# The first loads and transposes of a two-layer decoder step, put in another order on three queues

## What is computed

```python
q, k, v, z, xbc, dt = jnp.split(x @ w_in, IN_SPLITS, axis=-1)
dt = jax.nn.softplus(dt + dt_bias)
lam = jnp.exp(jnp.dot(lp[0], lp[1])) - jnp.exp(jnp.dot(lp[2], lp[3])) + lam_init
...
mk, mv = jnp.split(mem_prompt @ w_ckv[l], 2, axis=-1)
hp = _layer_norm(DEEPNORM_ALPHA * hp + _cross_attn(hp, mk, mv, w_cq[l], w_co[l]), ln_g[l, 1], ln_b[l, 1])
```

## Time and profile before

| | |
|---|---|
| median of 3 runs | 1859.1 us (1857.46 to 1862.97) |
| the profiled execution: its own time | 1857.33 us |
| its span, first to last instruction | 1855.5 us |
| mean granted TensorE clock | 0.969 |
| busy in the span: PE, DVE, ACT, POOL | 94%, 66%, 46%, 5% |
| DMA | 454 MB, mean 245 GB/s |

### The profile page before, as it was taken

One profiled execution on the slowest core, in us unless ns is written; L12 is line 12 of the kernel. 1 busy time (PEld: TensorE's weight loads), 2 busy tenths in 40 slices (PEclk: granted clock), 3 DMA queues, 4 the chain that ended last, 5 costly groups with the idle time before them and its releaser, 6 DMA issues.

```text
span 1855.5 us, 23939 instructions
## 1 busy us (share of the span) xinstructions
PE 1736.1 (94%) x8736; PEld 1355.2 (73%) x8736; DVE 1225.2 (66%) x1708; ACT 854.7 (46%) x978; POOL 100.1 (5%) x114
## 2 busy tenths in 40 slices
PE   7999997989998999998788999999999999999994
PEld 4646575689997555476477888888888888888883
DVE  2685627155543287534527979798988989797982
ACT  1122221054432131202115777676777777676762
POOL 0620000000000431000000000000000000000000
PEclk9999998999998999999898999999999999999996
DMA  9567536745535264553683989899999999998950
GB/s 323 169 213 237 220 123 242 254 137 182 171 117 194 91 217 148 214 200 115 241 255 125 351 263 368 307 356 335 332 359 316 362 313 380 296 367 308 354 208 26
DMA packets 298980, 454.07 MB, mean 245 GB/s; under 512 B 10710, under 2 KB 213648, under 8 KB 298886
## 3 DMA queue, kind: packets, MB, share of 16 engines
q1 hardware_dynamic: 294022, 440.47, 69.3%
q0 software_dynamic: 2576, 8.38, 1.5%
q10 hardware_dynamic: 2304, 4.20, 0.6%
HBM read 440.77 MB, written 12.38 MB: 244 GB/s over the span
## 4 chain that ended last, share of the span: by engine, by line
PE 86%; DVE 7%; ACT 3%; issue 1%; DMA 1%; SPq 1%; ACTq 0%; POOL 0%; DVEq 0%
PE bank L1142 83%; PE bank L1146 3%; DVE arena L2558 1%; DVE ring_low L2041 1%; ACT high L1669 1%; DMA out<-mem_rows 1%; ACT L1669 0%; ACT arena L1732 0%; ACT ye_high L1705 0%; DVE st L2530 0%; DVE st L2451 0%; DVE R L2172 0%; ACT xT L1768 0%; SPq L717 0%; DVE pair_in L2191 0%
## 5 line engine op out<-in xcount | busy, mean ns | idle before, releaser
L2041 DVE TENSOR_TENSOR ring_low<-ring,high 128x2048 fp32r<-128x2048 f32 x264 | 602.8, 2291 | 93.8 <-ACT high L1669 85.9
L1669 ACT ACTIVATE high<-ring 128x2048 fp32r<-128x2048 f32 x264 | 505.6, 1918 | 107.2 <-PE bank L1142 106.2
L1142 PE MATMUL bank<-high,xg_high 128*128 128x512 f32 x704 | 281.9, 400 | 8.7 <-DVE ring_low L2041 7.0
L1142 PE MATMUL bank<-ring_low,xg_high 128*128 128x512 f32 x704 | 275.1, 391 | 0.0
L1142 PE MATMUL bank<-high,xg_low 128*128 128x512 f32 x704 | 274.3, 390 | 0.0
L1142 PEld LDWEIGHTS bank<-high,xg_high 128*128 128x128 f32 x704 | 132.2, 188 | 35.1 <-DVE ring_low L2041 8.4
L1142 PEld LDWEIGHTS bank<-ring_low,xg_high 128*128 128x128 f32 x704 | 132.1, 188 | 28.6
L1142 PEld LDWEIGHTS bank<-high,xg_low 128*128 128x128 f32 x704 | 132.5, 188 | 25.3
L1732 ACT ACTIVATE arena<-bank 128x512 f32<-128x512 f32 (+3 forms) x95 | 47.4, 526 | 220.2 <-PE bank L1142 146.8
L1142 PE MATMUL bank<-high,he_high 128*128 128x512 f32 x352 | 139.7, 397 | 0.0
L1142 PE MATMUL bank<-ring_low,he_high 128*128 128x512 f32 x352 | 137.4, 390 | 0.0
(11 more groups left out here) (318 smaller groups left out, 2472.1 us busy)
## 6 DMA issues: line engine op xcount, KB each, us to landing
ring<-in_w_exp_gu SPq DMA_DIRECT2D x176, 1024.0 KB, 11.4
ring<-in_w_exp_down SPq DMA_DIRECT2D x40, 2048.0 KB, 14.0
ring<-in_w_in SPq DMA_DIRECT2D x12, 2048.0 KB, 11.8
ring<-in_w_ffn_gu SPq DMA_DIRECT2D x22, 1024.0 KB, 8.0
ring<-in_w_ckv SPq DMA_DIRECT2D x8, 2048.0 KB, 8.2
ring<-in_cache_mem_k SPq DMA_DIRECT2D x16, 1024.0 KB, 8.1
ring<-in_cache_mem_v SPq DMA_DIRECT2D x16, 1024.0 KB, 6.4
ring<-in_cache_attn_k SPq DMA_DIRECT2D x32, 256.0 KB, 4.2
```

Of the source, the lines that this page charges most:

```text
L1142: return M.matmul(out, lhsT, rhs, start=start, stop=stop)
L1669: S.activation(high_bufs[h % HIGH_BUFS][:], ring[:, s, j * HALF:(j + 1) * HALF], ACT.Copy).then_inc(split_high, 1)
L2041: V.tensor_tensor(ring_low[:, s, part], ring[:, s, part], high_bufs[h % HIGH_BUFS][:], ALU.subtract).then_inc(split_low, 1)
```

## The change

SP now loads the identity alone first (semaphore `ident_landed`), then x, then the q columns; the rest of the constants, the six vector DMAs, the memory rows and the page table follow behind q. The nine DMAs of `small_landed` are issued by POOL, the dt columns first, in front of its wait for `const_landed`. PE transposes x first, then `vraw`; the memory rows are transposed behind the two q tiles. The entries of `xin` are emptied by DVE (0, 2, 4) and ACT (1, 3). The memory rows' ring slot stands behind q's.

```diff
@@ psum_groups
-    g = [(("vec",), "V")]
-    g += [(("xin", n), "V") for n in range(5)] + [(("mem", n), "A") for n in range(4)]
+    g = [(("xin", n), "A" if n in (1, 3) else "V") for n in range(5)] + [(("vec",), "V")]
...
+                if l == 0 and c == "q" and t == DECODE_FIRST[-1]:
+                    g += [(("mem", n), "A") for n in range(4)]
@@ sync
-            sp.dma_start(const[:], a["consts"]).then_inc(const_landed, 16)
+            sp.dma_start(const[:, C_ID:C_ID + P], a["consts"][:, C_ID:C_ID + P]).then_inc(ident_landed, 16)
             s = rg.claim(sp, ("x",))
...
                 columns((l, "q"), w_in, 0)
                 if l == 0:
-                    for i, n in enumerate(("dt_bias", "a_log", "d_skip")):
-                        sp.dma_start(raw8[:, i], a[n].partition_broadcast(P)).then_inc(small_landed, 16)
...
+                    first_vectors()
+                    memory_rows()
@@ gpsimd
             G.memset(xpad[:, :, 0:3], 0.0).then_inc(buffers_set, 1)
+            for n in range(L):
+                pool.dma_start(wdt[:, n], a["w_in"][n, :, 3072:3080].rearrange("(k p) n -> p k n", p=P)
+                               ).then_inc(small_landed, 16)
+            for i, n in enumerate(("dt_bias", "a_log", "d_skip")):
+                pool.dma_start(raw8[:, i], a[n].partition_broadcast(P)).then_inc(small_landed, 16)
+            with nc.allow_non_contiguous_dma(reason="sixteen words"):
+                for i, n in enumerate(("dt_bias", "a_log")):
+                    pool.dma_start(col8[:, i, :], a[n].rearrange("l h -> h l")).then_inc(small_landed, 16)
+            pool.dma_start(lraw, a["lambda_params"].partition_broadcast(P)).then_inc(small_landed, 16)
+            pool.dma_start(wr[:], a["w_router"][0].rearrange("(k p) n -> p k n", p=P)).then_inc(small_landed, 16)
             pool.wait_ge(const_landed, 16)
@@ tensor
-            pe.wait_ge(const_landed, 16)
+            pe.wait_ge(ident_landed, 16)
+            blocks8(("xin",), slot(("x",))[:, 0:3072].rearrange("p (t n) -> p t n", t=3))
             pe.wait_ge(vecs_landed, 16 * 6)
             bk = turns.open(pe, ("vec",))
...
+            pe.wait_ge(const_landed, 16)
+            copied(pe, ("xin", 3))
             pe.wait_ge(buffers_set, 6)
...
+                    if l == 0 and c == "q":
+                        memory_columns()
```

More of the change, by code:

```diff
@@ L690, in _, with first_vectors, memory_rows @@
                          ).then_inc(landed[s], 16)
[L691 to L694, removed]
+            def first_vectors():
+                sp.dma_start(const[:, C_ID + P:NCONST], a["consts"][:, C_ID + P:NCONST]).then_inc(const_landed, 16)
+                for j, (src, r0) in enumerate((
+                        (a["ln_g"].rearrange("l i (k n) -> (l i k) n", n=P), 0),
+                        (a["ln_b"].rearrange("l i (k n) -> (l i k) n", n=P), 48),
+                        (a["ssm_norm_w"].rearrange("l (k n) -> (l k) n", n=P), 96),
+                        (a["attn_norm_w"], 104),
+                        (a["conv_b"].rearrange("l (k n) -> (l k) n", n=P), 106))):
+                    sp.dma_start(vraw[r0:r0 + src.shape[0], 0, :], src).then_inc(vecs_landed, 16)
+                sp.dma_start(vraw[0:64, 1, :], a["conv_w"].rearrange("l i (k n) -> (l i k) n", n=P)
+                             ).then_inc(vecs_landed, 16)
+            def memory_rows():
+                s = rg.claim(sp, ("mem",))
+                sp.dma_start(ring[:, s, 0:2048].rearrange("p (t n) -> p t n", t=2),
+                             a["mem_prompt"].rearrange("o (t p) n -> p (o t) n", p=P)).then_inc(landed[s], 16)
+                sp.dma_start(ptab[:], a["page_table"].rearrange("b g -> (b g)").unsqueeze(0)).then_inc(ptab_landed, 16)
             def columns(key, w, c0):
@@ L1235, in _, with memory_columns @@
             full(tr(bk[:, 128:192], vraw[0:64, 1, :], 64))
[L1236 to L1243, removed]
+            def memory_columns():
+                mem_in = slot(("mem",))[:, 0:2048].rearrange("p (t n) -> p t n", t=2)
+                for n in range(4):
+                    bk = turns.open(pe, ("mem", n))
+                    for j in range(4):
+                        k = 4 * (n % 2) + j
+                        last = tr(bk[:, j * P:(j + 1) * P], mem_in[:, n // 2, k * P:(k + 1) * P], P)
+                    full(last)
+            pe.wait_ge(const_landed, 16)
+            copied(pe, ("xin", 3))
             pe.wait_ge(buffers_set, 6)
@@ L1772, in _ @@
             S.preload_act_table_set(EXP_AND_LN)
-            for n in range(4):
-                copy_out(("mem", n), memT[:, 4 * (n % 2):4 * (n % 2) + 4, (n // 2) * P:(n // 2 + 1) * P],
+            for n in (1, 3):
+                copy_out(("xin", n), xT[:, 4:8, (n // 2) * P:(n // 2 + 1) * P],
                          lambda bk: bk[:].rearrange("p (k n) -> p k n", k=4))
@@ L1805, in _ @@
                             copy_out((l, "tok", name, t), qk_raw[:, t, 512 * c:512 * (c + 1)], lambda bk: bk[:])
+                    if l + c == 0:
+                        for n in range(4):
+                            copy_out(("mem", n), memT[:, 4 * (n % 2):4 * (n % 2) + 4, (n // 2) * P:(n // 2 + 1) * P],
+                                     lambda bk: bk[:].rearrange("p (k n) -> p k n", k=4))
                 decays_in.wait(act, l)
@@ L2194, in _ @@
             step.inc(V.memset(xs, 0.0))
-            bk = take(dve, ("vec",))
-            step.done(V.tensor_copy(pick[:], const[0:40, C_PICK:C_PICK + 8]))
-            step.inc(V.tensor_copy(vecT[:, 0, 0:122], bk[:, 0:122]))
-            emptied_after(("vec",), V.tensor_copy(vecT[:, 1, 0:64], bk[:, 128:192]))
-            for n in range(5):
+            for n in (0, 2, 4):
                 t, bk = n // 2, take(dve, ("xin", n))
@@ L2212, in _ @@
             decode_columns(0)
+            bk = take(dve, ("vec",))
+            step.inc(V.tensor_copy(vecT[:, 0, 0:122], bk[:, 0:122]))
+            emptied_after(("vec",), V.tensor_copy(vecT[:, 1, 0:64], bk[:, 128:192]))
+            dve.wait_ge(const_landed, 16)
+            step.done(V.tensor_copy(pick[:], const[0:40, C_PICK:C_PICK + 8]))
             dve.wait_ge(small_landed, 16 * 9)
```

28 lines of the change are left out of this document (7 added, 21 removed).

## The result

The changed kernel took 1869.35 us (median of 15 runs, 1865.07 to 1872.92) against 1859.1 us (15 runs on the same chip, 1854.09 to 1866.39): 10.2 us between the medians. The ratio, which is taken from all the runs, is 1.0043 with a 95% interval of 1.003 to 1.0056, or 8 us more (5.6 to 10.4). The forecast of 1860.0 us and its whole range were too low, and its likeliest case, no difference that can be measured, did not come about. The profiled execution took 1868.43 us with a span of 1866.7 us, 11.2 us more than the span before.

The account below looks back on a forecast made before the run. It took PE's unbroken work, starting at 21.67 us after the landing of `wr`, to bound the kernel. Earlier q tiles (-2.5 us) and uncovered memory transposes (+3.4 us) gave +0.9 us: 1860.0 us, range 1855.0 to 1865.5 us.

Parts of the forecast that it names:

- likeliest case: Whole program: time within 0.3% (5.6 us) of the kernel before; chance 0.80.
- The late landing of the small DMAs: At dt: PE waits for POOL's nine DMAs until 28.9 us, +10.7 us, 1869.8 us; chance of passing 0.3%: 0.14.
- The edits at nothing: DVE's earlier set-up of small vectors, the convolution state's later load and POOL's rotation chain: no cost to PE.
- I take 16.3 us: Head: the six vector DMAs, queued behind q, land at 16.3 us, leading to q's tiles 2.5 us earlier.
- the upper bound of 17.3 us: Vectors' landing with all 3.2 us of the small DMAs' work in front of them.
- the lower bound of 14.1: Vectors' landing if nothing else uses the DMA engines: 2.68 MB at 0.39 MB/us, 6.9 us after x.
- The clock term: q's tiles: the 1.2 us lost to half clock stays, taken as no difference; bounds -1.2 to +1.2 us.
- The memory rows' transposes: Between q's tiles and k's quarters: four groups, without a wait to hide behind, cost PE 3.4 us.
- The sum: At k's quarters: 2.5 us gained and 3.4 us lost, +0.9 us; bounds -2.5 to +3.1 us.
- the "faster" rival: Head bound by PE's own work: 3.1 us gained, 4.3 with full clock, 1854.8 us; counted within the 0.80.

Follow-up runs that it names:

- the changed kernel with dt late: Changed kernel with dt and its wait for the small DMAs moved behind q's two tiles, in both layers: 1859.13 us, ratio 0.9999.
- the runs with a known delay: Kernel before with extra identity transposes in front of k's quarters of layer 0: ratio 1.0027 with 48 transposes, 1.0062 with 96 transposes.
- the run with 48 transposes: Kernel before with 48 extra identity transposes in front of k's quarters of layer 0, no load moved: ratio 1.0027.
- the 40 transposes: Changed kernel with 40 extra identity transposes on PE between x and the wait for the vectors, no load moved: 1867.52 us, ratio 1.0047.
- the kernel before with dt late: Kernel before with dt and its wait for the small DMAs moved behind q's two tiles, in both layers: 1850.11 us, ratio 0.9953.

## Why the prediction was wrong

**Right.** x's transposes began at 7.20 us (forecast 7.26), and the requests' columns were copied at 12.09 us (12.4). PE then waited for `conv_w`, longer than ever there. The late landing of the small DMAs, the rival on the slower side, did not come about. This is POOL's timeline, where `wr` is the last of the nine, and then ACT's first work behind them:

```profile
7.29 0.93 POOL L873 DMA_DIRECT2D wr<-in_w_router  x1
```

```profile
17.39 0.21 ACT L1800 ACTIVATE raw<-raw 128x16 f32<-128x16 f32 x1 [5.91 <-DMA wr<-in_w_router]
```

They were in by 17.39 us, short of the 19.1 us at which they would have decided, and dt began without a wait. The edits at nothing cost nothing that the timeline shows.

**The step that failed: "I take 16.3 us" for the vectors.** They came at 20.79 us, 4.5 us later and 3.5 us past the upper bound of 17.3 us. That bound added POOL's 3.2 us of work whole to the queue's 6.9 us, and took for granted that what stands first in the queue lands first. Neither was a bound. Between 7 and 14 us the queue lost 3.4 us to POOL's packets, more than the 2.6 us that these themselves took, and 14 to 17 us were still below the rate (0.99 MB). By bytes alone the 2.70 MB (the forecast's 2.68 had the vectors' 186 rows of 512 bytes at 0.07 instead of 0.10 MB) would have been through near 18.0 us: 1.33 MB by 14 us, 0.99 MB by 17 us, and the rest at the 0.386 MB/us of the next 3 us. The last 2.8 us are order. By the packet sizes in the DMA view the last of the vectors' rows moved just before 19.5 us; by then q1 had moved 4.88 MB, 1.0 MB more than the 3.85 MB that stand in it up to the vectors' end. With the nine back on SP it was 13.7 us, 4.11 MB and 0.3 MB. (PE went on 1.3 us and 1.5 us after these last rows.) So POOL's packets cost both rate and order. That they do not slow all 16 DMA engines alike would explain the second; this is argued, as no view tells one DMA engine from another. Without POOL's packets the vectors came at 15.21 us, 1.1 us past the lower bound of 14.1.

The Trainium skill's rule that speaks against the step (DMA: Bandwidth & Descriptors, section on rules for kernel authors: other issuing engines bring no bandwidth, as all DMAs run on the same 16 engines) had the right sign: by it the forecast had 17.3 us, the run 20.79 us. The trace agrees with it and goes further: from 7 to 14 us both queues together moved 1.78 MB, where SP's queue alone moved 2.66 MB with the nine back on it.

**The clock term, "I take no difference".** q's quarters took 3.57 us to dt's start instead of 2.0, and dt with its tail 4.94 instead of 4.55 us: 2.0 us, above the bound of 1.2. The forecast had named the pause, but let it fall on the tiles alone; the pause of 9.0 us was also over twice the one expected (12.4 to 16.3 us).

**A term mis-sized the other way.** The memory rows' transposes were put at 3.4 us, from copies that ran while PE was at the rate of its first transposes; behind q's tiles they took 1.84 us. The two are the levels of the clock: in the changed kernel with dt late the same 16 transposes took 3.68 us, at a granted clock of 0.50, and in the changed kernel 1.91 us, at 1.00. That is 1.6 us won, and it hides the loss in the quarters.

**The sum.** Of the 4.7 us between the forecast 42.3 us for k's quarters and the measured 47.00, 4.5 are the vectors, 2.0 the clock and -1.6 the transposes, less 0.2 at the seams and in q's tiles. So the head lost 5.6 us where the forecast had 0.9. If these go to the end one for one, with which the runs with a known delay agree, 5.6 us is 0.30%, the lower end of the measured interval. The other 2.4 us, up to the ratio's 8, are within the interval, and that they belong to the change is not shown: in the profiled execution the growth behind the head is stretches at half clock between 115 and 593 us, of a kind that the run with 48 transposes has too. Nor does the head of one profiled execution put the runs in order: with the nine back on SP k's quarters were 6.6 us late and the time 3.5 us longer (0.6 to 6.5 us), with the 40 transposes 4.6 us late and 8.7 us longer (5.2 to 12.3 us). These two intervals just overlap; what makes the difference, if it is one, stays open.

The 1.2 us of low clock in q's tiles, on which the "faster" rival hoped, was the more interesting number: it pointed to dt's place, which was worth 8.7 us, and neither the change nor the forecast touched it.

## What to carry to other kernels

A DMA that is needed early should not stand behind megabytes in a queue that another queue disturbs: here it landed 2.8 us later than the bytes up to its end account for, and small DMAs on a second queue cost it 5.6 us. When work that cost nothing is moved away from the front, ask what PE does in its place: if it stands, the work behind it may run at half clock. Many small matmuls in front of large ones are worth trying behind them, in every layer.

## What the runs showed of the hardware

- q's quarters, 16 matmuls of 32 columns, took either 1.92 us or 3.2 to 3.64 us in layer 0, the two levels of the clock (2.4 and 1.2 GHz) in duration. In all eight kernels in which PE had stood for 3.76 us or more shortly before, they were slow; in three of the four with 0.7 to 0.9 us, and in the one with 40 transposes and 2.1 us, they were at full speed. The fourth is the kernel before with dt late, slow after 0.90 us, with the same instructions up to there as the kernel before. So the pause is not all that decides.
- The column of the granted clock reads 1.00 where its records have not begun: in the changed kernel the first one starts near 26 us. So it says 1.00 for 20 to 25 us, in which the quarters took 3.64 us. In the changed kernel with dt late the records reach back further, and the same stretch, with quarters of 3.58 us, has 0.50:

```profile
20.00:25.00 5.00, 4.21 (x18) 0.96 (x18) 3.12 (x28) 0.20 (x1) 1.10 (x2) 1.00 1.07 374
```

```profile
20.00:25.00 5.00, 3.87 (x18) 0.95 (x18) 2.77 (x24) 0.21 (x1) 1.10 (x2) 0.50 1.06 376
```

  (stretch, its length, busy time of PE, PEld, DVE, ACT and POOL, PEclk, DMA share, GB/s.) Durations of equal instructions are the better witness there.
- POOL's queue carried rows of 32 bytes in far fewer packets than SP's: q0 has 2912 packets in the whole changed kernel, and only 336 of them, 0.39 MB, moved between 7.2 and 20.8 us; under SP the small ones alone were 3632 packets. The 3072 rows of 32 bytes of `wdt` and `wr` went in 48 packets of 2 KB, 64 rows in each. Few packets are not cheap ones: 0.38 MB on q0 went with 1.33 MB less on q1.
